# A hybrid-attention stack with a two-stream block behind it: early loads, and the context prepared inside the last output units

## The reference

```
for layer in range(2):
    h = rms_norm(x, gain); proj = h @ w_in
    y_n = attention_n(...) @ w_branch[n]          # n = a, b, c
    x = x + (sum_n sigmoid(merge_n) * y_n) @ w_out
x = rms_norm(x, final_gain)
```

```
h   = rms_norm(x)   * g * (1 + sc)  + sh
h_c = rms_norm(ctx) * g * (1 + csc) + csh
p = [h; h_c] @ even_w_in                          # columns f, u and vs
```

## Time and profile before

| what | us |
|---|---|
| median of 3 runs | 1578.64 (1578.16 to 1579.22) |
| the profiled execution | 1579.09 |
| its span, first to last instruction | 1577.3 |
| PE busy in it | 1538.7 |

### The profile page before, as it was taken

One profiled execution on the slowest core, in us unless ns is written; L12 is line 12 of the kernel. 1 busy time (PEld: TensorE's weight loads), 2 busy tenths in 40 slices (PEclk: granted clock), 3 DMA queues, 4 the chain that ended last, 5 costly groups with the idle time before them and its releaser, 6 DMA issues.

```text
span 1577.3 us, 31432 instructions
## 1 busy us (share of the span) xinstructions
PE 1538.7 (98%) x13599; PEld 1472.3 (93%) x13599; DVE 1039.6 (66%) x1347; ACT 756.5 (48%) x1132; POOL 100.7 (6%) x79
## 2 busy tenths in 40 slices
PE   5999999999999999999999999999999999989999
PEld 5999999999999999899999999999999996889999
DVE  5878767578877775554456758886345347766674
ACT  4555554465465544653355322233245327655453
POOL 0311000003010000000020000000011002000000
PEclk9999999999999999999999999999999999989999
DMA  7676454566774546512035557754335224245854
GB/s 263 217 242 221 163 178 149 183 228 208 241 241 160 188 161 211 178 64 81 28 108 174 174 180 241 243 179 143 90 116 174 90 81 102 86 134 154 234 172 136
DMA packets 312333, 260.92 MB, mean 165 GB/s; under 512 B 24066, under 2 KB 298498, under 8 KB 312068
## 3 DMA queue, kind: packets, MB, share of 16 engines
q1 hardware_dynamic: 294260, 253.52, 49.6%
q10 hardware_dynamic: 17936, 5.40, 1.6%
HBM read 257.85 MB, written 1.05 MB: 164 GB/s over the span
## 4 chain that ended last, share of the span: by engine, by line
PE 54%; issue 7%; DVE 5%; ACT 3%; DMA 0%; POOL 0%; ACTq 0%; DVEq 0%; SPq 0%; POOLq 0%
PE banks_g L1417 34%; PE banks_g L967 7%; PE banks_g L1127 5%; PE banks_g L1276 2%; DVE w_lo L2498 1%; ACT near_p L2043 1%; DVE w_lo L2200 1%; PE banks_g L956 1%; ACT w_hi L1794 1%; PE banks_g L1378 1%; PE bank_s L1450 0%; POOL bias L2128 0%; PE bank_t L1464 0%; DVE near_max L2792 0%; PE bank_t L894 0%
## 5 line engine op out<-in xcount | busy, mean ns | idle before, releaser
L1417 PE MATMUL banks_g<-h_hi,w_lo 128*128 128x256 f32 x1296 | 360.5, 278 | 1.0 <-DVE w_lo L2498 0.6
L1417 PE MATMUL banks_g<-h_lo,w_hi 128*128 128x256 f32 x1296 | 358.5, 277 | 0.0
L1417 PE MATMUL banks_g<-h_hi,w_hi 128*128 128x256 f32 x1296 | 358.5, 277 | 0.0
L2498 DVE TENSOR_TENSOR w_lo<-raw,w_hi 128x2048 fp32r<-128x2048 f32 (+1 forms) x100 | 207.6, 2076 | 100.6 <-ACT w_hi L1794 100.3
L2200 DVE TENSOR_TENSOR w_lo<-raw,w_hi 128x2048 fp32r<-128x2048 f32 x92 | 212.4, 2310 | 72.5 <-ACT w_hi L1594 72.2
L1417 PEld LDWEIGHTS banks_g<-h_hi,w_lo 128*128 128x128 f32 x1296 | 243.5, 188 | 3.0 <-issue 0.9
L1417 PEld LDWEIGHTS banks_g<-h_hi,w_hi 128*128 128x128 f32 x1296 | 243.6, 188 | 0.0
L1417 PEld LDWEIGHTS banks_g<-h_lo,w_hi 128*128 128x128 f32 x1296 | 243.3, 188 | 0.1
L967 PE MATMUL banks_g<-h_hi,w_lo 128*128 128x256 f32 x800 | 226.0, 283 | 0.3 <-DVE w_lo L2200 0.3
L967 PE MATMUL banks_g<-h_hi,w_hi 128*128 128x256 f32 x800 | 221.4, 277 | 0.0
L967 PE MATMUL banks_g<-h_lo,w_hi 128*128 128x256 f32 x800 | 221.4, 277 | 0.0
(11 more groups left out here) (414 smaller groups left out, 3277.3 us busy)
## 6 DMA issues: line engine op xcount, KB each, us to landing
raw<-w_in SPq DMA_DIRECT2D x76, 1024.0 KB, 4.8
raw<-w_up SPq DMA_DIRECT2D x88, 512.0 KB, 4.9
ada_raw<-ada_w SPq DMA_DIRECT2D x24, 1024.0 KB, 7.1
raw<-w_down SPq DMA_DIRECT2D x32, 704.0 KB, 4.3
raw<-w_branch SPq DMA_DIRECT2D x12, 1024.0 KB, 4.9
ada_raw<-ada_t SPq DMA_DIRECT2D x12, 1024.0 KB, 4.9
late_raw<-ada_t SPq DMA_DIRECT2D x12, 1024.0 KB, 5.0
raw<-qkv SPq DMA_DIRECT2D x12, 1024.0 KB, 4.9
```

The source lines that it names most:

```text
L1417: last = nc.tensor.matmul(to, w[:, c, m0:m0 + P], a[:, c, s_ * SEQ:s_ * SEQ + SEQ], start=(m, s_, c, n) == (0, 0, 0, 0), stop=(m, s_, c, n ...
L2498: nc.vector.tensor_tensor(w_lo[:, u % SLOTS, 0:n], raw[:, u % SLOTS, 0:n], w_hi[:, u % SLOTS, 0:n].bitcast(F32), ALU.subtract).then_inc(dv ...
```

## The change

Six things are edited.

1. The opening's loads. `ident` and the vectors go to ACT's queue. SP loads x in two halves, unit 0 in two halves (`half_loaded` and slot 0's semaphore), and no longer waits before units 0 to 3, before the first ada load (now behind unit 1) and before `w_small` (now behind unit 2). The six constants move from ACT's queue to SP's, behind `w_small`.
2. The opening's work. PE waits for the vectors, then for each half of x. ACT does tanh and `s_cols` first, then x's conversions; unit 0 is converted and subtracted in halves, and PE starts its first four chunks on the first half (`half_lo`). ACT squares x in its untransposed form with a sum by row into `token_root1`; the sums on PE go in layer 0, where one product stands in their place. DVE reads x from PSUM in `x_low`, and copies `x_t` later.
3. The context's loads: two, behind units 40 and 41, the first after a wait for `values15`; the constants of the end part move behind END's unit 2.
4. The context's work moves into ORDER: `ctx prep` 0 to 3 behind units 39, 41, 42 and 43, `ctx turn` behind 43 and 44, `ctx h` behind 44 and 45, `ctx split` behind 44, 44, 45 and 47. Bank 3 of the turn becomes `bank_m`.
5. `final sums` (8 products, over squares that DVE has added further) is done inside vs 0 on the context, before chunk 6, and `spread00` inside vs 1 on the context, before chunk 4. The two jobs of vs on x run interleaved, chunk by chunk (`vs_x`).
6. Buffers: `conv`, `v_sum`, `late_sum`, `y_sq` and `last_sq` lie elsewhere, and 448 bytes are left free.

The diff, cut to its core:

```diff
         if n in (42, 43):
+            order.append(("ctx prep", n - 40))
             order += [("merged", 2 * (n - 42)), ("merged", 2 * (n - 42) + 1)]
+        if n in (43, 44):
+            order += [("ctx turn", 2 * (n - 43)), ("ctx turn", 2 * (n - 43) + 1)]
+        if n in (44, 45):
+            order += [("ctx h", 4 * (n - 44) + c) for c in range(4)]
+        order.extend(("ctx split", b) for b, at in enumerate((44, 44, 45, 47)) if n == at)
         if n >= 44:
 
             order.append(("x gain", n - 44))
             order.append(("squares", n - 44))
             order.append(("sums", n - 44))
-        order.extend(("ctx prep", m) for m, at in enumerate((41, 44, 44, 45)) if n == at)
+        if n == 39:
+            order.append(("ctx prep", 0))
+        if n == 41:
+            order.append(("ctx prep", 1))
         if n == 37:
...
+    order = [("final root",), ("second root",)]
...
+                    if layer or u >= SLOTS:
+                        sp.wait_ge(pe_steps, pe_.at(f"unit{before}", before=u < SLOTS))
+                        sp.sem_inc(sp_passed, 1)
...
+                    if (layer, u) == (0, 0):
+
+                        sp.dma_start(dst[:, 0:KC // 2, :], src[:, 0:KC // 2, :]).then_inc(half_loaded, 16)
+                        dst, src = dst[:, KC // 2:KC, :], src[:, KC // 2:KC, :]
                     sp.dma_start(dst, src).then_inc(raw_loaded[u % SLOTS], 16)
...
+                    if u in (40, 41) and layer == DEPTH - 1:
+
+                        t = u - 40
+                        if t == 0:
+                            sp.wait_ge(pe_steps, pe_.at("values15"))
+                        sp.dma_start(c_in[:, t, :], ins["ctx"][0, t * P:t * P + P, :]).then_inc(ctx_loaded[t], 16)
...
+                    if u == (1 if layer else 2):
+
+                        if layer:
+                            sp.wait_ge(pe_steps, pe_.at("small", before=True))
                         sp.dma_start(w_small[:, :, :], columns(K_IDX0, 80)).then_inc(small_loaded, 16)
+                        if layer == 0:
+
+                            for dst, src in ((rope[:, :, :], ins["rope"]), (causal[:, :, :], ins["causal"]),
+                                             (upto[:, :, :], ins["upto"]), (pick[:, :], ins["pick"]),
+                                             (add_parts[:, :], ins["add_parts"]),
+                                             (fbias[:, :, :].rearrange("p l h -> p (l h)"),
+                                              ins["forget_bias"].rearrange("(o l) h -> o (l h)", o=1
+                                                                           ).to_broadcast([P, DEPTH * 8]))):
+                                sp.dma_start(dst, src).then_inc(consts_loaded, 16)
...
+                    elif what == "ctx turn" and layer == DEPTH - 1:
+                        b, = arg
+                        if b == 0:
+                            pe.wait_ge(ctx_ready, 8)
+                            pe.wait_ge(dve_steps, dve_.at("masked15"))
+                            pe.wait_ge(act_steps, act_.at(f"turned15 {BATCHES[15][1]}"))
+                            pe.wait_ge(dve_steps, dve_.at("mod now"))
+                        for j in range(2):
+                            for t in range(2):
+                                last = nc.tensor.transpose(ctx_bank(b)[:, j, t * P:t * P + P],
+                                                           c_n[:, t, (2 * b + j) * P:(2 * b + j + 1) * P], ident[:, :])
+                        last.then_inc(ctx_turned, 1)
...
+            def final_sums():
+
+                pe.wait_ge(x_squared, 9)
+                for n, parts in ((2, y_sq[:, 0, :, :]), (0, last_sq[:, 0:2, :])):
+                    for t in range(2):
+                        for j in range(2):
+                            mm = nc.tensor.matmul(bank_o[:, SUM_COL + n + t:SUM_COL + n + t + 1],
+                                                  parts[:, j, t * P:t * P + P], ones[:, 0:1],
+                                                  start=j == 0, stop=j == 1)
+                mm.then_inc(pe_steps, pe_.step("final sums"))
+
...
+            def vs_ctx(i):
+
+                u = END_U[("vs", i)]
+                wh, wl = halves(u)
+                k = END_JOBS[("vs", i, 1)]
+                pe.wait_ge(first_lo, DEPTH * AHEAD + (u + 1))
+                bank_empty(k)
+                for c in range(KC):
+                    if i == 0 and c % 2 == 0:
+                        pe.wait_ge(ctx_split, c // 2 + 1)
+                    if (i, c) == (0, 6):
+                        final_sums()
+                    if (i, c) == (1, 4):
+                        spread00()
+                    for m in range(2):
+                        t0 = (2 + m) * P
+                        for n, (a, w) in enumerate(((h2_lo, wh), (h2_hi, wl), (h2_hi, wh))):
+                            last = nc.tensor.matmul(bank_g[k % BANKS][:, m * 256:m * 256 + 256], a[:, c, t0:t0 + P],
+                                                    w[:, c, :], start=(m, c, n) == (0, 0, 0),
+                                                    stop=(m, c, n) == (1, KC - 1, 2))
+                last.then_inc(pe_steps, pe_.step(f"job{k}"))
+
+            def vs_x():
+
+                ks = [END_JOBS[("vs", i, 0)] for i in range(2)]
+                pair = [tuple(halves(END_U[("vs", i)])) for i in range(2)]
+                for k in ks:
+                    bank_empty(k)
+                for c in range(KC):
+                    pe.wait_ge(dve_steps, dve_.at(f"x split{c}"))
+                    for i, (wh, wl) in enumerate(pair):
+                        for m in range(2):
+                            for n, (a, w) in enumerate(((h2_lo, wh), (h2_hi, wl), (h2_hi, wh))):
+                                last = nc.tensor.matmul(bank_g[ks[i] % BANKS][:, m * 256:m * 256 + 256],
+                                                        a[:, c, m * P:m * P + P], w[:, c, :],
+                                                        start=(m, c, n) == (0, 0, 0), stop=(m, c, n) == (1, KC - 1, 2))
+                        if c == KC - 1:
+                            last.then_inc(pe_steps, pe_.step(f"job{ks[i]}", f"unit{END_U[('vs', i)]}"))
+
...
+            cc = vec[:, ROWS["c"]:ROWS["c"] + 16].rearrange("p (s c) -> p s c", s=2)
+            nc.scalar.activation(s_f[:, :, :], cc, ACT.Tanh, scale=0.5).then_inc(act_steps, act_.step("s tanh"))
+            act.wait_ge(pool_steps, pool_.at("s cols"))
+            act.wait_ge(dve_start, 1)
+            for s in range(2):
+                nc.scalar.activation(s_cols[:, :, S_AT + s], s_f[:, s, :], ACT.Copy, scale=0.5
+                                     ).then_inc(act_steps, act_.step("s cols"))
...
+                if b % 2:
+                    n = b // 2
+                    act.wait_ge(raw_loaded[0] if n else half_loaded, 16)
+                    half = slice(n * UNIT // 2, (n + 1) * UNIT // 2)
+                    nc.scalar.activation(w_hi[:, 0, half], raw[:, 0, half], ACT.Copy
+                                         ).then_inc(act_steps, act_.step(f"first hi{n}"))
+            for t in range(2):
+                nc.scalar.activation(qk[0][:, 4 * t:4 * t + 4, :].rearrange("p a t -> p (a t)"), x_in[:, t, :],
+                                     ACT.Square, accum_out=token_root1[:, t:t + 1]
+                                     ).then_inc(act_steps, act_.step("x rows"))
+            act.wait_ge(raw_loaded[1], 16)
+            nc.scalar.activation(w_hi[:, 1, :], raw[:, 1, :], ACT.Copy).then_inc(act_steps, act_.step("hi1"))
...
+            for c in range(KC):
+                if c % 2 == 0:
+
+                    dve.wait_ge(act_steps, act_.at(f"x hi{c + 1}"))
+                x_low(c, vec[:, n:n + KC], x_banks[c // 2][:, c % 2, :])
+                if c % 4 == 3:
+                    half = slice(c // 4 * UNIT // 2, (c // 4 + 1) * UNIT // 2)
+                    dve.wait_ge(act_steps, act_.at(f"first hi{c // 4}"))
+                    nc.vector.tensor_tensor(w_lo[:, 0, half], raw[:, 0, half], w_hi[:, 0, half].bitcast(F32),
+                                            ALU.subtract).then_inc(first_lo if c // 4 else half_lo, 1)
+            for b in range(4):
+                nc.vector.tensor_copy(x_t[:, 2 * b:2 * b + 2, :], x_banks[b]).then_inc(dve_start, 1)
+                if b == 1:
+                    first_low(1)
...
-                            add_squares(i, layer * 3 + 2 + i)
-                        elif i < 3:
-                            add_squares(i, 4 + 2 * i)
+                            add_squares(i, i - 1)
+                        else:
+                            if i == 2:
+                                first_low(0)
+                            last_add(i, 1 + 2 * i)
                             nc.vector.tensor_tensor(y_sq[:, 0, :, :], y_sq[:, 0, :, :], y_sq[:, 1, :, :], ALU.add
                                                     ).then_inc(x_squared, 1)
+                            if i == 3:
```

(49 more changed lines are left out.)

225 lines of the change are left out of this document (71 added, 154 removed).

## The result

| | median us | range | ratio to before, 95% |
|---|---|---|---|
| before, same chip | 1578.93 | 1578.16 to 1579.84 | |
| changed | 1568.01 | 1565.96 to 1569.48 | 0.993 (0.9912 to 0.9947) |
| forecast | 1563.2 | 1560.3 to 1567.3 | |

Faster, by 10.9 us and not by 15.4; the median lies 0.7 above the range. The profiled execution took 1565.96 (its span is 1564.1), 13.1 less than the 1579.09 of before and 2.3 more than the 1563.7 that the sum gave for it.

The account below looks back on a forecast made before the run. TensorE, busy for 98% of the span, was taken as the bound, so only its waits, low clock or removed work pay. Opening 9.8 plus passage 5.6 gave 15.4 us off: 1563.7 profiled, 1563.2 median, range 1560.3 to 1567.3.

Parts of the forecast that it names:

- opening, up to the end of the branches: Opening: earlier loads and halved work start PE's first unit at 11.8 and second at 20.8, gaining 9.8 us.
- passage to the start of f, net: Last layer's outputs through vs to unit f: f starts at 698.0 instead of 703.68; 5.6 us gain taken.
- rival A: New idles before the context's turn and before f: PE's clock falls, 2.0 us a fall, 1565.3; chance 0.2.
- rival C: Opening gives more: PE's clock may rise sooner, by up to 2 us, 1561.3; chance 0.1.
- wait of 2.0: Last layer, before the context's turn: PE stands until 644.45 for ACT's second scaling, a new 2.0 us wait.
- f's chain: Before unit f: gelu, conversion 0.5 later taking 1.91, DVE's subtraction 2.29; PE waits 2.3 us.
- B: Opening falls short: x lands as late as now and DVE lags, gain 3 us smaller, 1566.3; chance 0.13.
- E: Early loads wait for something the trace doesn't show; only the passage gains, 1573; chance 0.04.
- D: End part: moved buffers' place in SBUF slows some 7,300 products behind f, 33 us lost, 1596; chance 0.03.

Follow-up runs that it names:

- vectors_first: Changed kernel with both new waits removed, plus identity and vectors issued at the head of SyncE's queue, before x: 1563.68 us, 0.9897.
- waits_restored: Changed kernel, but SyncE again waits for a free slot before units 0 to 3: 1574.15 us, 0.9965.
- prep_early: Changed kernel with the context's second scaling (ctx prep 3) directly behind the first, after unit 42: 1563.91 us, 0.9904.
- again: The changed kernel run again with no edit: 1567.38 us, 0.9922.
- changed_again: The changed kernel once more, unedited, on one chip with a version that has both new waits removed: 1569.08 us, 0.9927.
- x_on_act: Changed kernel with both new waits removed, identity and vectors heading SyncE's queue, then weights; x's halves on ScalarE's queue: 1563.19 us, 0.9895.

## Why the prediction was wrong

By its terms, in the profiled execution:

| term | forecast | measured |
|---|---|---|
| opening, up to the end of the branches | -9.8 | -9.36 (-9.06 at the second unit) |
| passage to the start of f, net | -5.6 | -4.86 |
| clock behind f | 0 | +1.6 |
| sum at `w_s` | -15.4 | -12.6 (714.7 to 702.1) |
| behind it | 0 | -0.5 |

**The step that failed is rival A, set at 0.2 and outside the sum.** It said that the clock falls in a new idle, and priced a fall at 2.0. Of the 2.8 by which the sum at `w_s` fell short, the clock is 1.6, the passage 0.7 and the opening 0.4. The median is only 0.7 above the range, so no single one of these is its whole cause; the clock is the largest, and the only one whose mechanism was known and argued away. Of three profiled executions of the changed kernel all have the fall before f (1.6 us each) and two also the one behind the turn (about 1: 51.1 and 50.7 from the context's turn to that of c_in, against 49.9). What I held against it, that full work follows both idles, is no reason. Over all profiled executions 8 of the 11 idles of 2.0 to 2.4 us at these two places were followed by slow products; none of the 3 filled ones was, and none of the 10 passes in which the wait was taken away. An idle of 1.9 was enough near 45 in vectors_first (9 of 12 with it), one of 1.3 at the same place wasn't in waits_restored, and one of 2.36 before f wasn't in prep_early. What decides in the single case isn't shown; for a forecast it is a chance by idle and execution, and had to stand in the sum at about 1 us each (my estimate: 9 in 12 of 1 to 1.6). The Trainium skill, "TensorE: Matmul & The Clock Gate", The HAM clock gate, says that the number of cold products at a kernel's start varies from run to run of one kernel. The traces here agree, and show it in the middle of one too: 9 to 24 slow products at one place near 1375 in kernels that don't differ there. That sentence was to be had before.

**The opening's term was too large by 0.7 at the second unit, 0.4 at the end of the branches.** The vectors were costed at the 4.2 us of the earlier trace rows, which they took beside the six constants; beside x they took 5.7. PE's first unit came at 13.00 instead of 11.8; 0.5 of the 1.2 came back, since its first products ran at 2.4 GHz (14 slow ones in the unit and not 19), which is rival C in small. What the forecast missed is which queue runs beside them, below. The weights' landing, the halves, the order on ACT, the absence of a stall inside unit 0 and the second unit's low half came as worked out.

**The passage was right in kind, 0.8 short in size.** The wait of 2.0 and the turn 0.2 after its forecast place; no stop and no slow products between the last output unit and vs; f's chain at 0.5, 1.9, 2.3 and a wait of 2.36 for 2.3. The 49 us from the turn to the gelu took 0.6 more than the sum.

**The median.** The remaining 2.0 between 1565.96 and 1568.01 lie between executions of one kernel: 15 of the changed kernel give 1567.72 (1565.56 to 1569.77), 34 of before 1579.51 (1576.55 to 1582.53). The gain over all of them is 11.8. The profiled execution of the changed kernel was near the best, with one fall of the two. The mean clock doesn't order them: of before, 1578.19 ran at 0.991 and 1582.53 at 0.992.

The three profiled executions of the changed kernel show four places where executions of it part: the fall at the turn (1.4 of slow products, or none), the slow stretch near 1375 (9 to 15 products), waits that differ by up to 0.7 each in the last 360 us, and the pace of the products at the full clock. That pace has two values, 0.1133 and 0.1177 us for one of 128x256. Here is a stretch of such products only, in the first execution and in `again`, with 87 of them in 10 us and then 91:

```profile
1358.00:1368.00 10.00, 10.00 (x87) 10.00 (x86) 7.67 (x10) 6.54 (x8) 0.00 (x0) 1.00 0.72 209
```

```profile
1358.00:1368.00 10.00, 10.00 (x91) 10.00 (x90) 7.76 (x10) 6.56 (x8) 0.00 (x0) 1.00 0.72 210
```

Over the whole run the first has 2114 at the slower pace (counted from start to start, 0.1155 to 0.122), `again` 1747 and changed_again 1743 (before: 1817). The 367 more are 1.6 us, which is why the first, with one fall fewer, has the same span. What sets the pace stays open, and so does where the unprofiled executions lose their 3 to 6 us.

Two slips in its sums change nothing: A, B and C are added to 1563.3 where the sum gives 1563.2, and 24 products at 0.21 from 11.8 end at 16.9 and not at 16.6. The rivals besides: B was not seen in the changed kernel, but was near (0.9 us to spare at logf, by the lines above, and vectors_first used them up). C was there in small, 0.5; E was not seen. D's loss was not either: the stretches behind f keep their length (`late_all` to the head's sums: 368.2 before and after). Its idea that the place in SBUF alone sets the pace doesn't hold, since one kernel shows both paces in the same stretch.

## What to carry to other kernels

A new idle of 2 us on a busy TensorE costs its own length and, in 9 of 12 cases here, 1 to 1.6 us by the lower clock behind it: put that in the sum, and look first for whether the wait can be removed by moving the producer ahead of its neighbour; both here could, by moving an entry in a list, for another 4 to 7 us. The vectors' load took 2.6 to 6.3 us, by what ran on the other queue; read a load's neighbours' traffic, not only its duration. And when an opening moves forward, follow each engine to the first place where its slack ends, some 25 us on.

## What the runs showed of the hardware

The vectors' load of 192 KB, always directly behind ident on its queue, took different times from issue to landing: 2.6 us with nothing on the other queue (x and the weights behind it on its own); 4.2 with the six constants on the other queue; 5.3 with x on ACT's queue and the vectors on SP's; 5.5 to 6.3 with x on SP's and the vectors on ACT's:

```profile
qk<-vectors ACTq DMA_DIRECT2D x1, 192.0 KB, 5.7
```

```profile
qk<-vectors SPq DMA_DIRECT2D x1, 192.0 KB, 2.6
```

```profile
qk<-vectors SPq DMA_DIRECT2D x1, 192.0 KB, 5.3
```

(changed kernel, vectors_first, x_on_act). So here the earlier load of one queue was served first, and loads of two queues shared. In waits_restored, where no weights run beside them, it is 5.5 against 5.7 to 6.3 in the nine other traces of that order: x does nearly all of it. The Trainium skill, "DMA: Bandwidth & Descriptors", Queues, rings and completion order, says that each DMA engine takes turns between the queues that have work; the times agree.

And a clock fall needs no long idle: 1.9 to 2.4 us were enough, in 9 of 12 cases.
